# A hybrid decoder layer on one core: slopes folded into the queries, softmax scaling moved to ScalarE, the value tile projected in quarters

## What is computed

```python
z = h @ w_in                                   # q, k, v of mixers A and B, index queries and key, gates
q, k = rms_norm(q) * g_q, rms_norm(k) * g_k    # per head of 64
s = sum_h relu(qi_h . ki / 8) * wi_h           # index scores; the 128 best keys of a query are kept (mixer A)
logits_A = q . k / 8 - slope_h * dist          # slope_h = 2**-(h+1), h = 0..7; masked and unselected: -1e30
logits_B = q . k / 8 + F_q - F_k               # F: running sum of the log forget values
o = softmax(logits) @ v
```

## Time and profile before

| | us |
|---|---|
| median of 3 runs | 1120.89 (1119.53 to 1124.39) |
| the profiled execution's own time | 1125.59 |
| its span, first to last instruction | 1123.4 |
| TensorE busy / VectorE / ScalarE / GpSimd | 1005.9 / 571.9 / 399.5 / 170.0 |
| before the loop | 0 to 79.9 |
| pass 0 | 79.9 to 121.57 |
| passes 1 to 8 | 121.57 to 413.53 |
| pass 9 and the end of the units | 413.53 to 431.2 |
| rest of the kernel | 431.2 to 1123.4 |

### The profile page before, as it was taken

How to read it: one execution, slowest core, us unless ns; L and a number is a source line. 1 busy time by engine, 2 the same in 40 slices (tenths; PEclk the granted TensorE clock), 3 DMA queues, 4 the chain that set the end, 5 groups by cost and what they waited for, 6 DMA issues and landing times.

```text
span 1123.4 us, 20111 instructions
## 1 busy us (share of the span) xinstructions
PE 1005.9 (90%) x7616; PEld 917.1 (82%) x7616; DVE 571.9 (51%) x1299; ACT 399.5 (36%) x803; POOL 170.0 (15%) x122
## 2 busy tenths in 40 slices
PE   8798878998899889549989999599989999998998
PEld 6596666887788778547389999489989999998998
DVE  3544799776575661554038844564433224443232
ACT  3344444444445442112064544443421113332111
POOL 3003222322342232230003232000000000000000
PEclk9899989998999899778979999799999999999999
DMA  9431521322121224783616665323222333332322
GB/s 351 135 82 33 158 76 48 87 57 57 47 76 48 59 57 120 231 270 121 235 57 206 189 205 176 89 57 94 85 75 87 91 93 94 93 91 71 90 66 76
DMA packets 184106, 124.54 MB, mean 111 GB/s; under 512 B 14419, under 2 KB 168083, under 8 KB 184036
## 3 DMA queue, kind: packets, MB, share of 16 engines
q1 hardware_dynamic: 183906, 123.50, 36.5%
q10 hardware_dynamic: 130, 0.10, 0.0%
HBM read 116.99 MB, written 6.59 MB: 110 GB/s over the span
## 4 chain that ended last, share of the span: by engine, by line
PE 79%; DVE 8%; DMA 4%; ACT 3%; issue 3%; POOL 2%; SPq 1%; ACTq 0%; DVEq 0%; POOLq 0%
PE bank L863 21%; PE bank L864 20%; PE bank L865 20%; DMA qbc<-q_d 3%; PE bank L968 2%; PE bank L945 2%; PE bank L954 2%; PE bank L1116 1%; POOL prod L770 1%; PE bank L782 1%; PE bank L1007 1%; PE bank L804 1%; PE bank L986 1%; DVE w_lo L1725 1%; PE bank L923 1%
## 5 line engine op out<-in xcount | busy, mean ns | idle before, releaser
L863 PE MATMUL bank<-h_hi,w_hi 128*128 128x260 f32 x1360 | 411.0, 302 | 32.9 <-DVE h_lo L1668 17.7
L864 PE MATMUL bank<-h_lo,w_hi 128*128 128x260 f32 x1360 | 400.1, 294 | 0.0
L865 PE MATMUL bank<-h_hi,w_lo 128*128 128x260 f32 x1360 | 399.1, 293 | 0.0
L863 PEld LDWEIGHTS bank<-h_hi,w_hi 128*128 128x128 f32 x1360 | 273.2, 201 | 50.0 <-issue 41.7
L864 PEld LDWEIGHTS bank<-h_lo,w_hi 128*128 128x128 f32 x1360 | 273.3, 201 | 0.2
L865 PEld LDWEIGHTS bank<-h_hi,w_lo 128*128 128x128 f32 x1360 | 272.6, 200 | 0.0
L740 POOL TENSOR_TENSOR w_lo<-raw,w_hi 128x1024 fp32r<-128x1024 f32 x44 | 104.8, 2381 | 420.5 <-ACT w_hi L1311 253.7
L863 PE MATMUL bank<-u_hi,w_hi 128*128 128x260 f32 x512 | 146.5, 286 | 7.7 <-DVE u_lo L2120 7.7
L2105 DVE TENSOR_TENSOR w_lo<-raw,w_hi 128x1024 fp32r<-128x1024 f32 x62 | 76.0, 1226 | 145.7 <-ACT w_hi L1543 145.7
L864 PE MATMUL bank<-u_lo,w_hi 128*128 128x260 f32 x512 | 146.0, 285 | 0.0
L865 PE MATMUL bank<-u_hi,w_lo 128*128 128x260 f32 x512 | 145.9, 285 | 0.0
(11 more groups left out here) (317 smaller groups left out, 1320.3 us busy)
## 6 DMA issues: line engine op xcount, KB each, us to landing
raw<-in_w_in SPq DMA_DIRECT2D x44, 512.0 KB, 3.7
raw<-in_w_ada SPq DMA_DIRECT2D x32, 512.0 KB, 4.0
raw<-in_w_up SPq DMA_DIRECT2D x32, 512.0 KB, 3.9
raw<-in_w_down SPq DMA_DIRECT2D x32, 512.0 KB, 3.9
ada<-in_w_ada SPq DMA_DIRECT2D x4, 2048.0 KB, 12.7
kv<-in_cache_k_b SPq DMA_DIRECT2D x16, 256.0 KB, 3.0
qbc<-q_d SPq DMA_DIRECT2D x16, 256.0 KB, 4.4
kv<-in_cache_k_a SPq DMA_DIRECT2D x16, 256.0 KB, 3.4
```

What stands on the lines that cost most here:

```text
L863: mm(out, hi[:, k, :], x_h, start=first and k == ks[0], stop=False)
L864: mm(out, hi[:, k, :], x_l, start=False, stop=False)
L865: end = mm(out, lo[:, k, :], x_h, start=False, stop=last and k == ks[-1])
```

## The change

Four parts. (1) Mixer A's slopes are powers of two: the query's gain is divided by the slope (`gq` has one column for mixer B and four for mixer A), so VectorE adds the bare distances to the scores, and the exponential multiplies by the slope again (`scale`, and the negated maximum times the slope). Line 1796 goes. (2) VectorE only takes the reciprocal of the sum (`inverse_sum`); ScalarE scales the row (`probs`), first thing in slot U+1. (3) The value tile is projected in quarters: k = 0 to 3 of half 0 in slot 4 and k = 4 to 7 in slot 5, half 1 likewise in slots 6 and 7. Its copies move to slots 5 and 7, and the split of the next key tile from slot 7 to slot 0 of the next pass. (4) Index scores go to two pairs of banks in turn (4, 5 and 6, 7), so a pair waits for the relus of the pair before the last. The two splits of pass 0 move from GpSimd to VectorE. New semaphores `inv_ready` and `gq_consts` are left out below.

```diff
--- before.py
+++ after.py
@@ -51,7 +51,8 @@
 SLOTS = 8
-HALVES_AT = [0, 1, 2, 3, 4, 6]
+HALVES_AT = [0, 1, 2, 3, 5, 7]
+FIRST_HALF_AT = [4, 6]
 T_GATE = T_PAIR + 3 * N_PAIRS
@@ -171,7 +172,7 @@
         g_col = new("g_col", [P, 2])
-        gq = new("gq", [P, 2])
+        gq = new("gq", [P, 5])
         gk_row = new("gk_row", [P, 2, HD])
@@ -217,6 +218,7 @@
         p_t = new("p_t", [P, 2, 2, QB, P])
+        gq_scale = sb("gq_scale", [P, 5], F32, place["at"])[0]
         place["at"] += 8192
@@ -493,6 +497,11 @@
+        def unit_slope(U):
+
+            m, c = pair_mixer(U // 8)
+            return SLOPES[2 * c + U % 2] if m else 1.0
+
         def ada_bank(g):
@@ -726,6 +735,13 @@
             pool.memset(s8[:, 11, :], 0.0).then_inc(s_consts, 1)
+            link(pool.memset(gq_scale[:, 0:1], QK_SCALE))
+            for hh in range(2):
+                for c in range(H // 2):
+                    last = pool.memset(gq_scale[64 * hh:64 * hh + 64, 1 + c:2 + c], QK_SCALE / SLOPES[2 * c + hh])
+                if hh == 0:
+                    link(last)
+            last.then_inc(gq_consts, 1)
@@ -744,8 +760,9 @@
             for p, s in ITERATIONS:
-                for i in split_at(p, s):
-                    rest_w(i)
+                if p:
+                    for i in split_at(p, s):
+                        rest_w(i)
                 if p < N_PAIRS and s in (2, 4):
@@ -891,16 +908,18 @@
-            def project(i, half):
-
-                if half == 0:
-                    pe.wait_ge(hi_ready, i + 1)
-                    pe.wait_ge(lo_ready, i + 1)
-                b = half + 4 * par(i)
-                if i >= 1:
-                    before = i - 1 if par(i - 1) == par(i) else i - 2
-                    pe.wait_ge(act_evac, act_evac_value(before, half))
-                half_tile(i, half, bank[b][:, 0:HALF]).then_inc(proj_done, 1)
+            def project(i, half, ks=range(NCH)):
+
+                if ks[0] == 0:
+                    if half == 0:
+                        pe.wait_ge(hi_ready, i + 1)
+                        pe.wait_ge(lo_ready, i + 1)
+                    if i >= 1:
+                        before = i - 1 if par(i - 1) == par(i) else i - 2
+                        pe.wait_ge(act_evac, act_evac_value(before, half))
+                end = half_tile(i, half, bank[half + 4 * par(i)][:, 0:HALF], ks, first=ks[0] == 0, last=ks[-1] == NCH - 1)
+                if ks[-1] == NCH - 1:
+                    end.then_inc(proj_done, 1)
@@ -1000,11 +1019,11 @@
                 qb, h = 1 + n // H, n % H
-                if n >= 2:
-                    pe.wait_ge(idx_relu, n)
+                if n >= 4:
+                    pe.wait_ge(idx_relu, n - 2)
                 for hh in range(2):
                     rows = slice(64 * hh, 64 * hh + 64)
-                    mm(bank[4 + hh][:, 0:width(qb)], q_idx[rows, h // 2, qb * P:(qb + 1) * P], ki2[rows, 0:width(qb)],
+                    mm(bank[4 + n % 4 + hh][:, 0:width(qb)], q_idx[rows, h // 2, qb * P:(qb + 1) * P], ki2[rows, 0:width(qb)],
                        start=True, stop=True).then_inc(idx_done, 1)
@@ -1052,8 +1071,13 @@
                 U = SLOTS * (p - 1) + s
-                if s in HALVES_AT and (p, s) < (N_PAIRS + 1, 4):
+                if s < 4:
                     project(T_PAIR + 3 * p + HALVES_AT.index(s) // 2, HALVES_AT.index(s) % 2)
+                elif p <= N_PAIRS:
+                    if s in FIRST_HALF_AT:
+                        project(T_PAIR + 3 * p + 2, FIRST_HALF_AT.index(s), range(4))
+                    else:
+                        project(T_PAIR + 3 * p + 2, HALVES_AT.index(s) % 2, range(4, NCH))
                 if p < N_PAIRS:
@@ -1354,8 +1378,13 @@
                 act.wait_ge(lg_ready, U + 1)
-                A(lg[:, U % 3, 0:w], lg[:, U % 3, 0:w], ACT.Exp, bias=stat[:, 8 + U % 8:9 + U % 8],
+                A(lg[:, U % 3, 0:w], lg[:, U % 3, 0:w], ACT.Exp, bias=stat[:, 8 + U % 8:9 + U % 8], scale=unit_slope(U),
                   accum_out=stat[:, 16 + U % 8:17 + U % 8]).then_inc(e_ready, 1)
+
+            def probs(U):
+                w = width(U % 8 // 2)
+                act.wait_ge(inv_ready, U + 1)
+                A(lg[:, U % 3, 0:w], lg[:, U % 3, 0:w], ACT.Copy, scale=stat[:, 26 + U % 2:27 + U % 2]).then_inc(p_ready, 1)
@@ -1372,12 +1401,13 @@
             def store_back(p, kd):
-                m = pair_mixer(p)[0]
+                m, c = pair_mixer(p)
+                col = 1 + c if m else 0
                 act.wait_ge(back_done, 2 * p + kd + 1)
...
                         act.wait_ge(s_done, 8 * (p - 1))
-                    A(q_fm[:, p % 2, :], bank[3][:, :], ACT.Copy, scale=gq[:, m:m + 1]).then_inc(back_read, 1)
+                    A(q_fm[:, p % 2, :], bank[3][:, :], ACT.Copy, scale=gq[:, col:col + 1]).then_inc(back_read, 1)
                 else:
@@ -1399,7 +1429,7 @@
                     act.wait_ge(smt_done, 1)
-                A(rbuf[:, n % 2, 0:w], bank[4 + n % 2][:, 0:w], ACT.Relu).then_inc(idx_relu, 1)
+                A(rbuf[:, n % 2, 0:w], bank[4 + n % 4][:, 0:w], ACT.Relu).then_inc(idx_relu, 1)
@@ -1448,6 +1478,8 @@
                 before = slot_before(p, s)
+                if 0 <= U - 1 < N_UNITS:
+                    probs(U - 1)
                 if before in SIDE:
@@ -1743,7 +1775,9 @@
             dve.wait_ge(small_landed, 16 * N_SMALL)
-            dve.tensor_scalar(gq[:, :], g_col[:, :], QK_SCALE, None, ALU.mult)
+            dve.wait_ge(gq_consts, 1)
+            dve.tensor_tensor(gq[:, 0:1], gq_scale[:, 0:1], g_col[:, 0:1], ALU.mult)
+            dve.tensor_tensor(gq[:, 1:5], gq_scale[:, 1:5], g_col[:, 1:2].to_broadcast([P, 4]), ALU.mult)
@@ -1790,12 +1824,9 @@
                 if m == 1:
-                    if U == 32:
-                        dve.wait_ge(stored, 64)
                     src = sel[:, sel_at[qb]:sel_at[qb] + w] if qb else dist[:, SEQ - P:SEQ]
-                    link(dve.tensor_scalar(abias[:, 0:w], src, SLOPES[2 * c + hh], None, ALU.mult))
                     dve.wait_ge(s_done, U + 1)
-                    link(dve.tensor_tensor_reduce(out[:, 0:w], s_bank[:, 0:w], abias[:, 0:w], 1.0, TAKEN, ALU.add, ALU.max, mx))
+                    link(dve.tensor_tensor_reduce(out[:, 0:w], s_bank[:, 0:w], src, 1.0, TAKEN, ALU.add, ALU.max, mx))
                 else:
@@ -1805,13 +1836,11 @@
                                                   ALU.add, ALU.max, mx))
-                dve.tensor_scalar(nm, mx, -1.0, None, ALU.mult).then_inc(lg_ready, 1)
-
-            def probs(U):
-                w = width(U % 8 // 2)
+                dve.tensor_scalar(nm, mx, -unit_slope(U), None, ALU.mult).then_inc(lg_ready, 1)
+
+            def inverse_sum(U):
                 dve.wait_ge(e_ready, U + 1)
-                link(dve.reciprocal(stat[:, 25:26], stat[:, 16 + U % 8:17 + U % 8]))
-                dve.tensor_scalar(lg[:, U % 3, 0:w], lg[:, U % 3, 0:w], stat[:, 25:26], None, ALU.mult).then_inc(p_ready, 1)
+                dve.reciprocal(stat[:, 26 + U % 2:27 + U % 2], stat[:, 16 + U % 8:17 + U % 8]).then_inc(inv_ready, 1)
@@ -1947,7 +1978,7 @@
                 if 0 <= U - 1 < N_UNITS:
-                    probs(U - 1)
+                    inverse_sum(U - 1)
                 if 0 <= U < N_UNITS:
```

2 lines of the change are left out of this document (added).

## The result

| | before | after |
|---|---|---|
| median (us) | 1122.88 (1119.53 to 1125.46, 5 runs) | 1110.99 (1106.80 to 1112.06, 5 runs) |
| ratio | | 0.9896, 95% interval 0.9872 to 0.9920 |
| profiled execution | 1125.59, span 1123.4 | 1111.2, span 1109.3 |
| loop, start of pass 0 to its end | 79.9 to 431.2 | 80.3 to 418.26 |

The change is faster, by 11.9 us (1%) and not by 41: the forecast of 1080 and its range (1060 to 1102) are both too low. The two profiled executions differ by 14.1 us in span. The loop has 13.3 of them; the rest of the kernel took 692.2 us after the loop, and 691.0 now. So nearly the whole difference lies in the loop, as the forecast had it.

The account below looks back on a forecast made before the run. TensorE, busy 90%, was taken to bound the kernel through its waits and lower clock. Gains of 13 + 3 + 7.5 + 20 = 43.5, less 2, gave 41 us: 1080 us forecast, range 1060 to 1102.

Parts of the forecast that it names:

- VectorE's relief: Passes 1 and 2: scalings and slope products leaving VectorE win 3 us, bounds 0 and 6.
- waits in passes 4 to 8: TensorE's waits for the transposition of the probabilities, 21.7 us, fall to 10.3, new key waits included.
- waits in passes 1 to 3: TensorE's waits beside the top-k rounds fall from 13.2 us to 8.9.
- waits in pass 0: TensorE's waits for index relus and the key fall from 10.0 to 2.5 us, 7.5 won.
- clock, all passes: TensorE's time at the lower clock costs 26 us, 2 more outside; 20 won, 8 kept, bounds 0 and 28.
- the matmuls themselves: TensorE's matmuls: the change takes none away and their number stays, so 0.
- Scaling on ScalarE ... Cost there 0: 64 more ScalarE activations, 33 us in all, hidden in slot 4 by 1.79 us of idleness before the exponential.
- ScalarE in the chain: Rival: reciprocal, scaling and exponential loop through two in-order queues, slower than before at 1140 us; chance 0.04.
- The queue of SyncE is not passed by anything ... 0: SyncE's DMA queue: only the weight load of the split moved to slot 0 is affected; cost 0.
- Quarters: Value projection in slots 4 to 7: fills TensorE's gaps, leaving 22 of 34.9 us of waits, 13 us won.
- a quarter costs 1.5: One quarter of the value projection takes TensorE 2.99/2 = 1.5 us, the number of matmuls unchanged.
- 30 to 31: Sign that the forecast is right: passes of 30 to 31 us.

Follow-up runs that it names:

- only_scale_on_scalar: The kernel before, with only the scaling of the probabilities moved to ScalarE, at the head of its slot: 1138.03 us, ratio 1.0134.
- side_first: The changed kernel, with ScalarE doing the copy of a side step before the scaling in each slot: 1100.13 us, ratio 0.9779 against before.
- both_orders: The changed kernel, with side copies before the scaling and pair 0's forget-sum broadcasts issued before pass 0's page loads: 1093.00 us, ratio 0.9724 against before.
- only_index_banks: The kernel before, with only the index scores put in two pairs of banks: 1118.50 us, ratio 0.9962.
- fbc_early: The changed kernel, with SyncE issuing pair 0's two forget-sum broadcasts before pass 0's page loads: 1100.87 us, ratio 0.9807 against before.
- late_on_vector: scale_late with the multiplication of the scaling back on VectorE behind the reciprocal: 1098.20 us, ratio 0.9780 against before.
- scale_late_before: The kernel before, with only the scaling moved to ScalarE, just ahead of the exponential: 1118.19 us, ratio 0.9971.
- scale_late: The changed kernel, with the early forget-sum broadcasts and ScalarE's scaling just ahead of the exponential: 1086.23 us, ratio 0.9657 against before.
- joint: scale_late, with VectorE's reciprocal ahead of the forget-sum block and the top-k search's end in quieter slots: 1083.70 us; again 1083.80.
- scale_late_again: The unchanged kernel of scale_late run once more, beside joint on one chip: 1085.49 us, ratio 0.9669 against before.
- key_early: scale_late, with VectorE taking the key's mean squares before slot 4's logits and normalizing a slot earlier, from pass 1: 1102.98 us.

## Why the prediction was wrong, and where it was right

Idle and busy time of TensorE and the clock, summed from the stretches views of both kernels, put a measured size beside each term. The clock's term is (1 - clock) times the length, as in the forecast (before: 0.98 in pass 0, 0.89 in passes 1 to 3, 0.93 in 4 to 8 and 0.90 in pass 9). The forecast's 8.9 for passes 1 to 3 has its 3 us for VectorE's relief in it.

| term | forecast | measured |
|---|---|---|
| waits in passes 4 to 8 | 21.7 to 10.3 | 21.7 to 10.6 |
| waits in passes 1 to 3 | 13.2 to 8.9 | 13.3 to 24.7 |
| waits in pass 0 | 10.0 to 2.5 | 9.9 to 3.2 |
| clock, all passes | 20 won | 12 won (27.5 to 15.5) |
| the matmuls themselves | 0 | 5.1 lost |

The measured column gives 11.1 - 11.4 + 6.7 + 12.0 - 5.1 = 13.3, the loop's own difference (351.3 to 338.0 us). The 5.1 is what the others leave over, so all rounding sits in it; the clock has two digits, and 0.005 of the loop is 1.8 us. Of the 24.7 in passes 1 to 3, 11.6 are the three waits found above. The other 13.1 stand against 11.9 forecast without the relief: the new waits that the quarters bring there were priced about right.

**The step that failed: "Scaling on ScalarE ... Cost there 0".** It named what is queued behind the wait for the reciprocal as the rounding, the projection's copy and the exponential, and priced slot 4 of a pass like 6. Two things were missing. The side copy, which was first in its slot, is queued behind the wait as well, and TensorE needs it at once. And the time at which VectorE answers was taken from a pass like 6, where nothing precedes the reciprocal; in slot 0 of pass 2 a top-k round and the forget-sum block do, and in pass 3 the end of the search besides, which puts the scaling 4.4 us after the end of the exponential. The argument against the rival "ScalarE in the chain" was that ScalarE idles half of every pass; it does, and only_scale_on_scalar was 16.0 slower all the same, near the 19 of this rival, which had a chance of 0.04. Its mechanism is not the one that the rival described, a loop too long for every slot: 11.6 us of the loss lie in passes 2 and 3. In the change this step cost about 11 us, by side_first, and some 18 together with the next one, by both_orders.

The Trainium skill (TensorE: Matmul & The Clock Gate, Engine queue depths) says that ScalarE and VectorE take their queues strictly in order; the traces agree: the copy at 205.08 ran behind the scaling, after 4.08 us of standing still, and in side_first, where it stands ahead, TensorE does not wait for it.

**"The queue of SyncE is not passed by anything ... 0"** was the second failure. True of the code, but the end of pass 0 moves against that queue. The forecast had 7.5 us won in pass 0 and never asked which transfer pass 1 needs at its start. only_index_banks won 9.9 there and kept 3.5; fbc_early, which only moves the two broadcasts, was 10 faster than the change.

**"I add 3 us" for VectorE's relief** was mis-sized in the other direction: with the quarters in place late_on_vector puts it at 12.0, part of it clock. In the kernel before it is 3.1 (scale_late_before). In the change it could not be seen, since the waits of the two paragraphs above lie over it. The parts do not add up either: alone, the banks won 3.5, the quarters 15.3, and the scaling lost 16.0, 2.8 together, where the change won 11.9.

**The clock** was right where its condition held. In passes 5 to 8 the waits are 0.93 us and less, in pass 9 one is 1.47, and the granted clock is 1.00, the higher level (2.4 GHz) throughout; the new waits of pass 6 are 0.42, 0.41 and 0.43 us where 0.5, 0.8 and 0.4 were forecast, plus one of 0.40 for `o_lo` that was not. In passes 1 to 3 it is 0.88, as low as before (0.89), behind waits of up to 4.3 us. The Trainium skill (TensorE: Matmul & The Clock Gate, A second HAM failure mode: psum-queue depth-cycling) tells of a kernel in which frequent small idle times between groups of matmuls made the clock swing. If it were so here, the clock would have swung in passes 5 to 8; the trace does not agree, it has 1.00 there.

**Quarters** were right in the waits and slightly off in "a quarter costs 1.5". The stretches view of two quarters and a half tile in pass 6 of after:

```profile
328.50:330.20 1.70, 1.70 (x14) 1.49 (x12) 1.43 (x5) 0.82 (x4) 1.70 (x1) 1.00 0.00 0
331.79:333.50 1.71, 1.71 (x14) 1.50 (x12) 1.21 (x5) 1.35 (x5) 0.61 (x1) 1.00 0.98 264
320.71:323.86 3.15, 3.15 (x27) 3.02 (x25) 2.83 (x9) 0.88 (x4) 2.04 (x2) 1.00 0.40 109
```

A stream that stops in a wait shows its last matmul's full length, which the profile models: 1.70 and 1.71, against 3.15, which is 0.26 more for a split half. From the first start to the start of what follows without a wait, a half tile takes 2.99 (320.71 to 323.70), and 12 of its steps at that pace with the slower first one make a quarter 1.54: 0.1 more for a split half. For the 18 split halves this makes an estimate of 1.8 to 4.7 us of the 5.1. The rest is not explained. Passes 5 to 7 take 31.7 to 32.1 us and not the "30 to 31" of the forecast, which its own sum did not give either: for pass 6, 35.84 less 1.9 for the waits and 2.5 for the clock is 31.4.

**Right as they stood**: VectorE 35 to 45 us less busy (40.7), the slopes at nothing by themselves (0.6), pass 0 near 34 (32.8), no VectorE operation of 2 us in the loop (the longest takes 1.85; `probs` on ScalarE lasts 0.40 to 0.73), and later stages that shift as a whole. ScalarE rose by 28.3 for 33 forecast.

The Trainium skill (Trainium Architecture — The Big Picture, The five engines, in one table) advises against simple arithmetic on ScalarE, VectorE being up to about three times as fast per element. One scaling has a median of 563 ns on ScalarE (line 1387) against 420 on VectorE, a factor of 1.3, so the direction agrees. The time of the kernel went the other way: scale_late is 12 us faster than late_on_vector.

What was left of the gain is there to be had: the change with two orders altered (scale_late) runs at 1086, within 6 of the forecast, and joint, the best version tried, at 1083.8, 3.4% under before.

## What to carry to other kernels

When an operation that waits is put at the head of an in-order queue, list everything behind it until its consumers, side work too, and look up the answering engine's queue at its fullest place, not in a typical pass; half an idle engine says nothing about order. When a stage is made shorter, list what its successor needs at its first instruction, DMAs above all, and when each is issued. Undo such a part by moving it, before judging the part: here the same instructions cost 16 us at the head of the slot and saved 3 further back in it. And a part measured alone is not its share of the whole: look at it beside the others.

## What the runs showed of the hardware that was not expected

The clock's answer to a wait is not the same from one execution to the next. In scale_late and in scale_late_again, which are one kernel, the transposition waits the same 2.38 us in pass 3 (until 188.69 and 190.32). The half tile that follows, in the stretches view of the first and of the second:

```profile
191.18:196.12 4.94, 4.94 (x28) 4.94 (x27) 0.00 (x0) 0.28 (x1) 2.36 (x1) 0.59 0.21 56
```

```profile
191.68:194.82 3.14, 3.14 (x28) 3.14 (x27) 0.37 (x2) 1.42 (x2) 1.58 (x1) 1.00 0.28 80
```

Mostly the lower level in the one, only the higher in the other. In pass 2 it is the other way round: both executions have a wait of 2.33 us there for the key, and the pass takes 34.2 us at a clock of 1.00 in scale_late and 35.6 at 0.95 in scale_late_again. So a wait of 2 us can be followed by either level, as the earlier trace rows showed between them, and a single profile does not price it. Nor is 2 us a limit: pass 6 of key_early, at 0.91, has no wait above 1.7, and its pass 5 has two waits of the same lengths (0.96 and 1.69) at 1.00.

One VectorE operation of the search's end, 0.69 us in the change (202.07 above), takes 2.74 in scale_late and 2.75 in scale_late_again. In both a GpSimd subtraction started just before it; in scale_late (timeline, VectorE and GpSimd):

```profile
182.53 2.74 DVE L1816 SCALAR_TENSOR_TENSOR sel<-sel,dist 128x512 f32<-128x512 f32 x1
...
182.07 2.65 POOL L758 TENSOR_TENSOR w_lo<-raw,w_hi 128x1024 fp32r<-128x1024 f32 x1 [12.87 <-ACT w_hi L1337]
```

It ends 0.55 us after the subtraction does; the pair of the earlier trace rows ended 0.08 apart. In the change the subtraction starts at 206.74, after the operation is over. The change took the scalings out of GpSimd's way, but not this operation: a shift of a queue by some microseconds decides whether it is hit.
